# Second low-rank stage of decay and rate: four f32 matmuls replaced by three fp32r products of rounded parts and remainders

## What is computed

```python
wd = zf[..., o:o + R_DECAY]; o += R_DECAY      # 64 columns
ad = zf[..., o:o + R_AAA]; o += R_AAA          # 64 columns
w = -jax.nn.softplus(-(f32(w0) + jnp.tanh(wd) @ f32(w2))) - 0.5
decay = jnp.exp(-jnp.exp(w))
a = jax.nn.sigmoid(f32(a0) + ad @ f32(a2))
...
y = wkv7_scan(rh, heads(decay), kh, vh, -kk, kk * ah)
```

## Time and profile before

| | us |
|---|---|
| median of 3 runs (lowest, highest) | 2432.05 (2431.84, 2432.23) |
| profiled execution, whole | 2433.57 |
| its span in the trace | 2431.6 |
| PE busy in it | 2405.7 (99%) |
| DVE busy | 1130.9 (47%) |
| ACT busy | 781.5 (32%) |
| POOL busy | 194.6 (8%) |

### The profile page before, as it was taken

How to read it: one execution, slowest core, us unless ns; L and a number is a source line. 1 busy time by engine, 2 the same in 40 slices (tenths; PEclk the granted TensorE clock), 3 DMA queues, 4 the chain that set the end, 5 groups by cost and what they waited for, 6 DMA issues and landing times.

```text
span 2431.6 us, 42088 instructions
## 1 busy us (share of the span) xinstructions
PE 2405.7 (99%) x16524; PEld 2035.3 (84%) x16524; DVE 1130.9 (47%) x1733; ACT 781.5 (32%) x1321; POOL 194.6 (8%) x240
## 2 busy tenths in 40 slices
PE   8999999999999999999999999999999999999997
PEld 8999999999998788888888888888888888888886
DVE  7557657657657643533233333333332333333353
ACT  6533434434434322332222222221321322222333
POOL 5001101001001222000000000000000000000032
PEclk9999999999999999999999999999999999999999
DMA  8244244244244532333233233333233332333232
GB/s 251 77 99 102 70 99 102 69 104 100 69 104 111 185 109 82 100 102 90 87 104 95 84 108 95 88 101 90 87 104 87 93 107 80 103 102 88 87 100 91
DMA packets 487454, 243.67 MB, mean 100 GB/s; under 512 B 83295, under 2 KB 481121, under 8 KB 486881
## 3 DMA queue, kind: packets, MB, share of 16 engines
q1 hardware_dynamic: 470064, 219.99, 32.7%
q0 software_dynamic: 6720, 18.45, 2.3%
q10 hardware_dynamic: 10496, 2.62, 0.6%
HBM read 224.08 MB, written 16.92 MB: 99 GB/s over the span
## 4 chain that ended last, share of the span: by engine, by line
PE 90%; DVE 7%; ACT 1%; issue 1%; DMA 0%; SPq 0%; ACTq 0%; DVEq 0%
PE PD L1497 68%; PE PD L1502 13%; PE PD L1711 1%; DVE uni L1145 1%; DVE uni L1271 1%; PE PD L1526 1%; DVE w_lo L1050 1%; PE PW L1526 1%; PE PW L1673 1%; PE PW L1575 0%; DVE uni L1149 0%; PE PW L1581 0%; PE PW L1579 0%; PE PW L1637 0%; PE PW L1679 0%
## 5 line engine op out<-in xcount | busy, mean ns | idle before, releaser
L745 ACT CAST w_hi<-w_raw 128x512 fp32r<-128x512 f32 x780 | 456.8, 618 | 702.2 <-PE PD L1497 517.5
L1050 DVE TENSOR_TENSOR w_lo<-w_raw,w_hi 128x512 fp32r<-128x512 f32 x780 | 545.9, 732 | 292.3 <-ACT w_hi L745 288.7
L1497 PE MATMUL PD<-act_lo,w_hi 128*128 128x512 f32 x1344 | 531.3, 395 | 0.0
L1497 PE MATMUL PD<-act_hi,w_hi 128*128 128x512 f32 x1344 | 529.0, 394 | 0.0
L1497 PE MATMUL PD<-act_hi,w_lo 128*128 128x512 f32 x1344 | 528.6, 393 | 0.0
L1497 PE MATMUL PD<-u_hi,w_hi 128*128 128x512 f32 x1024 | 409.7, 400 | 0.0
L1497 PE MATMUL PD<-u_hi,w_lo 128*128 128x512 f32 x1024 | 403.3, 394 | 0.0
L1497 PE MATMUL PD<-u_lo,w_hi 128*128 128x512 f32 x1024 | 401.5, 392 | 0.0
L1497 PEld LDWEIGHTS PD<-act_hi,w_hi 128*128 128x128 f32 x1344 | 252.5, 188 | 61.2 <-issue 0.9
L1497 PEld LDWEIGHTS PD<-act_lo,w_hi 128*128 128x128 f32 x1344 | 252.1, 188 | 58.3 <-issue 0.2
L1497 PEld LDWEIGHTS PD<-act_hi,w_lo 128*128 128x128 f32 x1344 | 252.8, 188 | 57.3
(11 more groups left out here) (314 smaller groups left out, 1869.6 us busy)
## 6 DMA issues: line engine op xcount, KB each, us to landing
w_raw<-in_w_up SPq DMA_DIRECT2D x256, 256.0 KB, 3.1
w_raw<-in_w_down SPq DMA_DIRECT2D x256, 256.0 KB, 2.9
w_raw<-in_w_in SPq DMA_DIRECT2D x200, 256.0 KB, 3.2
w_raw<-in_w_out SPq DMA_DIRECT2D x64, 256.0 KB, 2.8
residual<-res POOLq DMA_DIRECT2D x2, 2048.0 KB, 10.2
out<-rows SPq DMA_DIRECT2D x8, 512.0 KB, 5.3
yin<-mixed POOLq DMA_DIRECT2D x15, 256.0 KB, 3.7
x_rows<-in_x SPq DMA_DIRECT2D x3, 1024.0 KB, 7.3
```

The lines of the kernel that those rows point to most:

```text
L745: nc.scalar.copy(w_hi[:, q % RING], w_raw[:, q % RAW]).then_inc(hi_split, 1)
L1050: V.tensor_tensor(w_lo[:, q % RING], w_raw[:, q % RAW], w_hi[:, q % RING].bitcast(F32), ALU.subtract).then_inc(lo_split, 1)
L1497: ins = M(pd_seq(n), w, v[:, k, first:first + SEQ], start=begin, stop=end)
```

## The change

The low-rank inputs and their matrices are split like the large operands. `low_wa` gets a rounded part by ACT (`low_wa_hi`) and a remainder by DVE (`low_wa_lo`), once, before pair 0. `wa_w` gets them by POOL, once a pair, straight behind its load (`split_wa`). `low` becomes twelve fp32r matmuls in place of four f32 ones. Two buffers move: `low_wa` lies where `AMV` is written later, and `wa_w` lies where `k_tok` is, so that ACT waits for the split before it writes `k_tok`.

```diff
+    over_pairs = ExitStack()
+    low_wa = sb("low_wa", [P, T], on=over_pairs)
+    over_pairs.close()
     AMV = m_sb("AMV", [P, 2, SLOTS, P])
...
+    over_k = ExitStack()
+    wa_w = sb("wa_w", [P, P], on=over_k)
+    over_k.close()
     k_tok = m_sb("k_tok", [P, SLOTS, P])
...
+    low_wa_hi, low_wa_lo = low_r("low_wa_hi", T), low_r("low_wa_lo", T)
+    wa_hi, wa_lo = low_r("wa_hi", P), low_r("wa_lo", P)
...
+        def split_wa(j):
+            pool.wait_ge(wa_loaded, 32 * (j + 1))
+            nc.gpsimd.tensor_copy(wa_hi[:], wa_w[:]).then_inc(wa_rounded, 1)
+            pool.wait_ge(wa_rounded, j + 1)
+            nc.gpsimd.tensor_tensor(wa_lo[:], wa_w[:], wa_hi[:].bitcast(F32), ALU.subtract).then_inc(wa_split, 1)
...
             if not last:
                 pool.wait_ge(pe_done, step(PE_STEPS, "low", j))
+                pool.wait_ge(wa_split, j + 1)
                 load_wa(j + 1)
...
+            if not last:
+                split_wa(j + 1)
             pool.wait_ge(dve_done, step(DVE_STEPS, "gram0", j))
...
         load_wa(0)
         load_g(0)
+        split_wa(0)
...
-                nc.scalar.activation(low_wa[0:HS, :], low_wa[0:HS, :], ACT.Tanh).then_inc(low_done, 1)
+                nc.scalar.activation(low_wa[0:HS, :], low_wa[0:HS, :], ACT.Tanh).then_inc(low_sig, 1)
+                act.wait_ge(low_sig, 2)
+                nc.scalar.copy(low_wa_hi[:], low_wa[:]).then_inc(low_top, 1)
...
                     done("btok", nc.scalar.copy(b_tok[:].rearrange("p c n -> p (c n)"), in_row(0)))
+                    if not last:
+                        act.wait_ge(wa_split, j + 2)
                     done("ktok", nc.scalar.copy(k_tok[:].rearrange("p c n -> p (c n)"), in_row(1)))
...
+                dve.wait_ge(low_top, 2)
+                V.tensor_tensor(low_wa_lo[:], low_wa[:], low_wa_hi[:].bitcast(F32), ALU.subtract).then_inc(low_done, 1)
...
                 if name == "low":
-                    pe.wait_ge(wa_loaded, at(32, 32, j))
+                    pe.wait_ge(wa_split, j + 1)
                     dve("ssm")
                     for a in range(2):
-                        for h in range(2):
-                            ins = M(PW[:, 2 * h + a, 0:HALF], wa_w[hs[h], :], half(low_wa[hs[h], :], a), start=True, stop=True)
+                        for i, (w, v) in enumerate(((wa_hi, low_wa_hi), (wa_lo, low_wa_hi), (wa_hi, low_wa_lo))):
+                            for h in range(2):
+                                ins = M(PW[:, 2 * h + a, 0:HALF], w[hs[h], :], half(v[hs[h], :], a), start=(i == 0), stop=(i == 2))
```

More of the change, by code:

```diff
@@ L273, in hybrid_layer @@
     cu = m_sb("cu", [P, T + 2])
-    low_wa = m_sb("low_wa", [P, T])
     low_r = lambda name, n: sb(name, [P, n], F32R, on=mix)
     low_hi, low_lo, low_tail = low_r("low_hi", SEQ), low_r("low_lo", SEQ), low_r("low_tail", SEQ)
-    wa_w = m_sb("wa_w", [P, P])
+    low_wa_hi, low_wa_lo = low_r("low_wa_hi", T), low_r("low_wa_lo", T)
+    wa_hi, wa_lo = low_r("wa_hi", P), low_r("wa_lo", P)
     g_w = m_sb("g_w", [P, P])
@@ L347, in hybrid_layer @@
     wa_loaded, g_loaded = sem("wa_loaded"), sem("g_loaded")
+    wa_rounded, wa_split = sem("wa_rounded"), sem("wa_split")
     low_done, low_sig, low_top = sem("low_done"), sem("low_sig"), sem("low_top")
@@ L814, in _ @@
                 nc.scalar.activation(low_g[:, META:T], low_g[:, META:T], ACT.Sigmoid).then_inc(low_sig, 1)
-                act.wait_ge(low_sig, 2)
+                act.wait_ge(low_sig, 3)
                 nc.scalar.copy(low_hi[:], low_g[:, META:T]).then_inc(low_top, 1)
@@ L1109, in _ @@
                 V.tensor_tensor(low_tail[r, :], low_g2[r, META:T], low_tail[r, :].bitcast(F32), ALU.subtract).then_inc(low_done, 1)
+                dve.wait_ge(low_top, 2)
+                V.tensor_tensor(low_wa_lo[:], low_wa[:], low_wa_hi[:].bitcast(F32), ALU.subtract).then_inc(low_done, 1)
             if n == 4:
-                dve.wait_ge(low_top, 2)
+                dve.wait_ge(low_top, 3)
                 V.tensor_tensor(low_lo[:], low_g[:, META:T], low_hi[:].bitcast(F32), ALU.subtract).then_inc(low_done, 1)
```

## The result

| | before | after |
|---|---|---|
| median, us (12 runs each) | 2431.94 (2430.97 to 2432.98) | 2438.69 (2435.7 to 2441.43) |
| ratio of the two | | 1.0027, 95% interval 1.0019 to 1.0034 |
| profiled execution, whole / span | 2433.57 / 2431.6 | 2435.7 / 2433.6 |

The change makes the kernel slower by 6.8 us, or 0.28% by the two medians. The forecast was +2.7 us, or 2434.75, and its range ended at 2437.6. The spread is a result too: the kernel before stays within 2 us, the changed one within 6.

The account below looks back on a forecast made before the run. PE was taken as the bound (busy 99%, 90% of the chain), with DVE setting the stretch around `low` in pairs 1 to 7. -0.3 + 3.0 = +2.7 us on the median 2432.05 gave 2434.75 us; range 2431.0 to 2437.6.

Parts of the forecast that it names:

- The output projection and the MLP are the same work: Behind the pairs: both are bound by PE and pass on the pairs' difference of +2.7 us.
- the sum that lists what the edit executes: Whole kernel: -0.3 us from `low` in pair 0 and +3.0 from POOL's split make +2.7 us.
- Rival C: Between L1148 and L1155 of pairs 1 to 6, the split holds DVE longer: at 1.0 us a pair, 2437.75; chance 0.08.
- POOL's split costs DVE 0.5 us a pair: Beside DVE's scan and small instructions before L1155, pairs 1 to 6: six times 0.5 us, +3.0 us.
- the share of 0.78: Part of POOL's time that DVE loses: 0.67 of a masked copy's 0.857 us; of the split's 0.75, 0.58.
- rival A: Beside DVE before L1155, the split costs under 0.3 us a pair: 2431.75 to 2433.55 us; chance 0.22.
- POOL's two take over 1.2 us together: Sign that the prediction is wrong: POOL's cast and subtraction in the split exceed 1.2 us, where 0.75 was estimated.
- `low` gains 0.3 us, only in pair 0: Twelve fp32r records take 0.8 us for 1.09: -0.3 us in pair 0, 0 in pairs 1 to 7.
- Rival B: `low` gains 0.3 us in all eight pairs and no split disturbs DVE: 2429.65 us; chance 0.06.
- D: `low`'s products don't run side by side: 1.43 us for 1.09, +0.35 in pair 0, 2435.4 us; chance 0.04.
- Work before pair 0 and the new waits cost nothing: ACT's cast and DVE's subtraction, some 0.7 us each, hide in idle time; added waits are already met: 0.
- The range's upper end: Whole kernel: 2437.6 us, said to be the forecast's at 0.93 us lost a pair.

Follow-up runs that it names:

- the split alone: The kernel before with POOL's split added into two buffers that nobody reads, PE's program unchanged: 2433.15 us, ratio 1.0003.
- Two products: The changed kernel with the third product of `low` (rounded matrix by remainder of the input) left out: 2432.64 us, ratio 1.0001.
- eight instructions: The kernel before with two of the four f32 matmuls of `low` executed twice in pair 0 only: 2433.37 us, ratio 1.0005.

## Why the prediction was wrong

- **"The output projection and the MLP are the same work ... and pass the difference on", and the sum that lists what the edit executes**: this step failed. The instructions are the same work, but they are not in the same place. Sixty-four more of them put the end of the MLP loop just behind the start of a block (+2.3 us by the medians with and without), and moved the block fetches in the pairs onto the exchange through DRAM, whose copy then landed after up to 4.6 us in place of 2.9. I read the diff's effect on PE as "only the step itself is longer" and had no rival in which that length counts. Rival C, with 2437.75 us, came nearest to the measured time, but its mechanism isn't what the runs show: that is luck.
- **POOL's split costs DVE 0.5 us a pair**: right in kind, wrong in size. Six pairs lost 0.55 us in all with the split alone, 0.1 a pair. In the change's first profile `ss` to `tr` was longer by 0.07, 0.13, 0.13, 0.14, 0.40 and 0.11 us, together 0.98, within which the 0.40 is a pair in which the load had landed 1 us sooner and POOL's two instructions met a `w_lo` (0.83 us in place of 0.69) and L1171 (0.69 in place of 0.43). The term that was too large is the share of 0.78, taken from rows 9. There, DVE's next long instruction of two inputs began inside POOL's copy. Here the scan, begun first, made POOL wait 0.8 us, and what followed it on DVE was short and of one input. This is rival A, which I had at 0.22. One of the signs named was "POOL's two take over 1.2 us together"; they took 1.6 in five of the six pairs.
- **`low` gains 0.3 us, only in pair 0**: right in kind, too large. The twelve records took 0.94 us rather than 0.8, side by side as assumed, and the gain in pair 0 is 0.10 us rather than 0.3. In the other pairs the waits before `gram0` grew in its place, from 0.26 to 0.57 us, where 0.56 was predicted; part of that is the split's. Rival B (the gain in each pair) and D (no overlap) are out.
- **Work before pair 0 and the new waits cost nothing**: right as far as it can be seen. Two products, with all of that work in, is equal to the kernel before.
- **The range's upper end** of 2437.6 is said to be the forecast's at 0.93 us a pair; it is that at 0.98, since 2432.05 - 0.3 + 6 x 0.93 is 2437.3. Nothing changes by it.
- **The sum by the measured terms**, were the program not displaced: -0.10 + 0.55 to 0.98 is +0.4 to +0.9 us, or 2432.4 to 2432.8 from the median of 2431.94. The measured excess of 6.8 is then 0.4 to 0.9 from the change's own work, 2.3 from the MLP loop, and some 3.6 to 4.1 that I put down to the pairs' displaced fetches. The last number is a remainder: the single profiles of kernels with all pairs displaced show 0.2 to 2.4 us of it between `tr` and `t16` of pairs 0 to 6, and perhaps 1.0 more in pair 7.

What stays open: the pairs' part was shown in place and kind in single profiles, and reproduced in pair 0 with eight instructions, but it varies from run to run, and no experiment kept three products with PE's program undisplaced. That a fetch beside it delays the copy rests on the times at which both run, without exception in 104 pairs; by what way, no row shows, nor why only half of the late copies cost PE time. Why the loop is fetched again at 225 to 233 and 33 and not at 101 and 163, and why 33 costs the most, was not found out either; no other places were tried.

No version beats the kernel before: the change's gain is 0.10 us in one pair of eight.

## What to carry to other kernels

An edit that changes the number of instructions of an engine with a long program moves everything behind it; at an effect of a few tenths of a per cent, compare with the same number of instructions, added or taken away, before the edit itself is given the credit or the blame. Added instructions aren't free of cost either: doubled matmuls cost 2.0 us here and 64 met waits 3.3, which had to be taken off first. Look for idle time that ends in "issue" at the return of a loop, and for the times of instruction transfers beside small transfers that someone waits for. When two engines block each other, ask which one starts first and what the other one has next in its queue; the length of the intruder alone gives only an upper bound.

## What the runs showed of the hardware that was not expected

- Instruction blocks of 16.4 kB are fetched again in each trip of the MLP loop of 1,632 instructions when its last instruction lies at 225 to 233 or at 33 of a block (145 or 146 blocks in the run), and not at all in it at 101 and 163 (92 blocks). At 33 PE is short of instructions for 0.1 to 0.8 us at three to five of the six returns, at 225 to 233 for 0.1 at a few, at 101 and 163 never.
- With an instruction block fetched between 0.2 us before and 2.1 us after its issue, a DRAM copy of 80 kB landed after 3.3 to 4.9 us (38 cases), otherwise after 3.0 at most (66 cases). SP's issue of the next load took 1.82 us in place of 0.64 in one such moment. A displacement by 8 instructions, 512 bytes, was enough to bring this about in one pair, which took 0.68 us more.
- Sixty-four instructions that only wait for something long met cost 3.27 us on PE in one place. Twenty-four ahead of pair 0 and 38 ahead of the MLP cost 0.4 us or less where a term for them could be read.
- fp32r matmuls of 64 rows in both halves of the array run side by side: twelve of 264 columns in 0.94 us.
- POOL and DVE: a DVE instruction of one input took 0.69 us in place of 0.43 beside POOL's subtraction of 128 x 128; a scan begun before the subtraction made POOL wait 0.8 us and took 1.31 to 1.38 us in place of 1.26.
